# Seven block products in place of eight in both feed-forwards of a one-core transformer kernel

## The chip, the core and the metric

One core of a Trainium2 chip runs the whole program. The metric is the device time of one execution in microseconds; lower is better.

## The reference, cut to what matters

Two stages work on x of 512 tokens by 1024 columns in float32: two layers with three kinds of attention, a short convolution and gates, then a block with a feed-forward, a mixer with dilated and block-selected attention, cross attention over 256 memory rows, and a second feed-forward. The change touches the two feed-forwards alone (D_FF is 2816):

```python
def swiglu(x, w_gu, w_down):
    gu = x @ w_gu
    g, u = jnp.split(gu, 2, axis=-1)
    return (jax.nn.silu(g) * u) @ w_down

x = x + 0.5 * swiglu(rms_norm(x, g_ffn1[layer]), w_ffn1_gu[layer], w_ffn1_down[layer])
```

## The kernel before

Activations lie transposed: 128 partitions hold 128 columns of the model, and the free axis the 512 tokens. A matrix of weights is a stream of slots of 128 x 1024 words (eight blocks of 128 x 128), loaded by SyncE into a ring of four slots. Each float32 value is held as a rounded high part and a low part (the rest), and each product of two matrices is three matmuls: high by high, high weights by low values, low weights by high values (products, L1006; the matmul is L1013). ScalarE rounds a slot into whi (make_high, L1736), VectorE or GpSimd subtracts to get wlo in place in the ring (make_low, L2201 on VectorE, L759 on GpSimd).

A feed-forward (ffn, L1398 on TensorE, L1998 on ScalarE, L2601 on VectorE) has 44 up jobs, g and u in turn for each of 22 chunks of D_FF: eight chunks of 128 model columns, three matmuls of 512 tokens each, summed in one of two PSUM banks (proj). VectorE scales g by the norm's factor R (L2285), ScalarE takes the tanh (L2007), VectorE makes the gate (L2624), multiplies by u out of the bank (L2628) and by R (L2631); ScalarE rounds the result (inner_hi, L2010), VectorE makes inner_lo (L2642). Then 8 down jobs sum 22 chunks of inner each and are added to xT with a factor of 0.25 (residual, L2279). Squares of xT for the next norm go to ScalarE (L1732) and their sum to GpSimd (L771). GpSimd has no weights to split in the feed-forwards: on_pool names only slots of the layers and of the mixer.

Each engine runs its own list of instructions in order and waits on counters (semaphores) that others raise: job_done when a job's last matmul ends, job_free when its bank has been read, lo_ready when the low part of the weights is there. Jobs alternate between the two banks, so the reading of one bank lies beside the next job, which takes 5.4 us. SyncE reloads a ring slot when the job that used it is done (slot_used, L622).

## Time and profile before

| | before |
|---|---|
| time, median of 3 runs | 1786.37 us (1785.3 to 1786.94) |
| profiled execution, span | 1785.4 us |
| TensorE busy | 1776.4 us (99%) |
| VectorE busy | 1062.3 us (59%) |
| ScalarE busy | 750.5 us (42%) |
| GpSimd busy | 407.3 us (23%) |
| DMA | 165.53 MB, mean 93 GB/s |

The profile is of one execution. Busy time of an engine is the time in which it had an instruction under way; a matmul's recorded duration is longer than the distance from one start to the next, since they are pipelined. PE is TensorE, DVE is VectorE, ACT is ScalarE, POOL is GpSimd, SP is SyncE.

### The profile page before, as it was taken

What the parts mean: (1) busy time and instruction counts of PE and PEld (TensorE: products, weight loads), DVE (VectorE), ACT (ScalarE), POOL (GpSimd) and SP (SyncE); (2) the same over time, 40 slices, a digit from 0 to 9 for tenths busy, and PEclk for the clock granted to TensorE, in tenths of its full rate; (3) what the DMA queues carried; (4) which work ended last, traced back from release to release, by engine and by line L of the source; (5) the groups of instructions that cost most, each with busy time, mean ns of one, the idle gap of its engine ahead of it and who ended that gap; (6) DMA issues with size and microseconds to landing.
All of it is one profiled execution on the core that took longest, in us unless ns stands there. A gap on an engine that the chain in (4) does not pass through costs nothing.

```text
span 1785.4 us, 25187 instructions
## 1 busy us (share of the span) xinstructions
PE 1776.4 (99%) x9274; PEld 1437.2 (80%) x9274; DVE 1062.3 (59%) x2106; ACT 750.5 (42%) x1386; POOL 407.3 (23%) x248
## 2 busy tenths in 40 slices
PE   9999999999999999999999999999999999999998
PEld 7767778776777888888888878879888888888887
DVE  5888777588877665445433445555756654555333
ACT  6464654446454533223222455545444322232222
POOL 4544553455354310000000232220200200000000
PEclk9999999999999999999999999999999999999999
DMA  5422222322212343333333422323321333333332
GB/s 188 125 81 70 60 59 85 97 81 83 67 53 60 96 138 102 95 94 94 106 106 104 150 60 83 95 72 107 95 73 55 92 101 94 94 94 101 99 106 94
DMA packets 49765, 165.53 MB, mean 93 GB/s; under 512 B 5640, under 2 KB 6152, under 8 KB 49672
## 3 DMA queue, kind: packets, MB, share of 16 engines
q1 hardware_dynamic: 48376, 161.47, 30.2%
q10 hardware_dynamic: 1296, 2.84, 0.4%
q8 instruction: 56, 0.92, 0.2%
q14 instruction: 37, 0.30, 0.1%
HBM read 162.12 MB, written 2.17 MB: 92 GB/s over the span
## 4 chain that ended last, share of the span: by engine, by line
PE 97%; DVE 1%; ACT 1%; issue 0%; POOL 0%; DVEq 0%; POOLq 0%
PE proj L1013 78%; PE turned L1302 2%; PE o L1326 2%; PE score L1276 2%; PE turned L1530 1%; PE proj L1460 1%; PE o L1556 1%; PE score L1521 1%; PE proj L1453 1%; PE score L1285 1%; PE o L1652 1%; PE turned L979 1%; PE score L1641 1%; PE score L1163 0%; PE proj L991 0%; PE turned L998 0%
## 5 line engine op out<-in xcount | busy, mean ns | idle before, releaser
L1013 PE MATMUL proj<-hhi,whi 128*128 128x512 f32 x1456 | 580.2, 399 | 0.6 <-DVE tanh L2285 0.3
L1013 PE MATMUL proj<-hhi,wlo 128*128 128x512 f32 x1456 | 568.1, 390 | 0.0
L1013 PE MATMUL proj<-hlo,whi 128*128 128x512 f32 x1456 | 567.3, 390 | 0.0
L1736 ACT ACTIVATE whi<-ring 128x1024 fp32r<-128x1024 f32 x279 | 295.2, 1058 | 622.7 <-PE proj L1013 614.4
L2201 DVE TENSOR_TENSOR wlo<-ring,whi 128x1024 fp32r<-128x1024 f32 x199 | 243.1, 1222 | 164.8 <-ACT whi L1736 164.5
L1013 PEld LDWEIGHTS proj<-hhi,whi 128*128 128x128 f32 x1456 | 274.3, 188 | 59.4 <-issue 6.6
L1013 PEld LDWEIGHTS proj<-hhi,wlo 128*128 128x128 f32 x1456 | 273.4, 188 | 58.8
L1013 PEld LDWEIGHTS proj<-hlo,whi 128*128 128x128 f32 x1456 | 274.0, 188 | 52.8
L759 POOL TENSOR_TENSOR wlo<-ring,whi 128x1024 fp32r<-128x1024 f32 x80 | 194.7, 2435 | 372.6 <-ACT whi L1736 372.0
L771 POOL TENSOR_TENSOR prob<-prob 128x512 f32<-128x512 f32 x36 | 56.6, 1574 | 873.9 <-ACT prob L1732 873.9
L1762 ACT ACTIVATE prob<-prob,negmax 128x256 f32<-128x256 f32 (+3 forms) x208 | 114.4, 552 | 65.5 <-DVE negmax L2274 64.1
L1013 PE MATMUL proj<-inner_hi,whi 128*128 128x512 f32 x352 | 136.9, 389 | 0.0
L1013 PE MATMUL proj<-inner_lo,whi 128*128 128x512 f32 x352 | 136.9, 389 | 0.0
L1013 PE MATMUL proj<-inner_hi,wlo 128*128 128x512 f32 x352 | 136.9, 389 | 0.0
L2274 DVE CUSTOM_DVE_ANT_0 prob<-score,arena 128x256 f32<-128x256 f32 (+3 forms) x208 | 92.7, 482 | 62.1 <-PE turned L1530 55.3
L2285 DVE TENSOR_TENSOR tmp<-proj,R 128x512 f32<-128x512 f32 x48 | 33.2, 691 | 121.1 <-PE proj L1013 118.8
L1013 PE MATMUL proj<-yhi,whi 128*128 128x512 f32 x245 | 96.7, 395 | 0.1
L1013 PE MATMUL proj<-yhi,wlo 128*128 128x512 f32 x245 | 95.6, 390 | 0.0
L1013 PE MATMUL proj<-ylo,whi 128*128 128x512 f32 x245 | 95.3, 389 | 0.0
L2628 DVE TENSOR_TENSOR tmp<-tmp,proj 128x512 f32<-128x512 f32 x44 | 30.3, 689 | 103.7 <-PE proj L1013 103.5
L1943 ACT ACTIVATE pT<-turned 128x128 f32<-128x128 f32 (+3 forms) x96 | 38.5, 434 | 102.8 <-PE turned L1302 102.1
L1013 PEld LDWEIGHTS proj<-inner_lo,whi 128*128 128x128 f32 x352 | 66.1, 188 | 13.8
(334 smaller groups left out, 2426.1 us busy)
## 6 DMA issues: line engine op xcount, KB each, us to landing
ring<-wstream SPq DMA_DIRECT2D x287, 512.0 KB, 3.6
arena<-lines SPq DMA_DIRECT2D x28, 256.0 KB, 5.5
arena<-x ACTq DMA_DIRECT2D x4, 512.0 KB, 5.9
out<-arena SPq DMA_DIRECT2D x8, 256.0 KB, 2.9
arena<-mem SPq DMA_DIRECT2D x1, 1024.0 KB, 9.4
ring<-wstream ACTq DMA_DIRECT2D x2, 256.0 KB, 7.3
arena<-hot SPq DMA_DIRECT2D x2, 80.0 KB
par<-params ACTq DMA_DIRECT2D x2, 74.0 KB, 1.9
```

What stands on the lines that cost most here:

```text
L759: return pool.tensor_tensor(rounded(wlo[:, s, :]), ring[:, s, :], whi[:, h, :], ALU.subtract)
L771: pool.tensor_tensor(sq[:, 3, :], sq[:, 0, :] if c == 1 else sq[:, 3, :], sq_last if c == KC - 1 else sq[:, c % 3, :], ALU.add).then_inc(s ...
L1013: mm = pe.matmul(b, rounded(w), rounded(rhs(v, k)), start=(first and n == 0 and p == 0), stop=(last and n == len(blocks) - 1 and p == 2))
L1276: mm = pe.matmul(score[b][:, 0:W], rounded(q_part[rows, pair, q]), rounded(k_part[rows, pair, 0:W]), start=first, stop=last)
L1302: mm = pe.transpose(turned[g % 2][:, kb * P:(kb + 1) * P], prob[:, (2 * s + n) % 4, kb * P:(kb + 1) * P], ident[:, :])
L1326: mm = pe.matmul(opsum[o % 2][h * HD:(h + 1) * HD, qb * P:(qb + 1) * P], v, pT[:, (g - 1 + h) % 4, kb * P:(kb + 1) * P], start=(kb == 0), ...
L1736: act.activation(rounded(dst), src, ACT.Copy, scale=scale).then_inc(ready, 1)
L1762: act.activation(prob[:, i, 0:W], prob[:, i, 0:W], ACT.Exp, bias=negmax[:, i:i + 1], scale=-1.0, accum_out=rowsum[:, i:i + 1] if total is ...
L1943: act.activation(pT[:, g % 4, 0:W], turned[g % 2][:, 0:W], ACT.Copy).then_inc(turn_out, 1)
L2201: dve.tensor_tensor(rounded(wlo[:, s, :]), ring[:, s, :], whi[:, h, :], ALU.subtract).then_inc(lo_ready, 1)
L2274: dve.tensor_tensor_reduce(prob[:, i, 0:W], src[:, 0:W], bias, 1.0, 3e38, ALU.add, ALU.min, negmax[:, i:i + 1]).then_inc(min_ready, 1)
L2285: return dve.tensor_tensor(dst, src, factors, ALU.mult)
```

## The change

Each feed-forward keeps its first four weight pairs (g and u of chunks 0, 4, 1, 5) as eight jobs of the old kind. The other 18 pairs and all of the down matrix go through 30 blocks, each a product of a 2 x 2 block matrix of weights (two slots) by a 2 x 2 block matrix of values: the tokens are cut into two halves of 256 (TS), the chunks of the summed axis into two halves. An up block has g and u of one chunk as its two rows and four chunks in each half; a down block has two output chunks as its rows, and 8, 8 or 6 of the 22 inner chunks as its summed axis (three parts, each four blocks). Such a product needs seven block products on sums of blocks where the plain form needs eight; each is 12 matmuls of 256 tokens (9 in the last part). In order they are the 1st, 7th, 6th, 4th, 5th, 2nd, 3rd:

- into bank R0 go the 1st, then on top the 6th, the 5th and the 3rd; into R2 the 7th and on top the 4th; into R1 the 2nd. Each bank has two copies, used by blocks in turn. Between two products of one bank its partial sum is read: r0_out counts these readings (after the 1st, after the 6th, after the 5th, after the 3rd), r2_p7_out and r2_out those of R2, r1_out that of R1.
- in an up block ScalarE copies the sums out after the 1st, 7th and 6th product (c1, c7, c2) and VectorE adds: gsum = c1 + R1, tmp = c7 + R0 and tmp = c2 + R2. In a down block VectorE adds each partial sum into xT (x_add, seven times 256 columns).
- for each block GpSimd makes four sums of weights of 512 columns and the low part of the slot of u (1024); ScalarE rounds g (1024), u (1024), two sums together (1024) and one more (512); VectorE makes the low parts of g in two halves (a_low), of the two sums (s12_low) and of the last one (s4_low).
- the values need sums of blocks too: for the normalised input once per feed-forward, on VectorE, GpSimd and ScalarE beside the first four pairs; for inner, when both chunks of a pair are there (pair_of), three sums on VectorE (512, 256, 256 columns), one rounding on ScalarE and one low part on VectorE of 7 x 256 columns each. This comes in 9 of the 18 up blocks and in the first down block of the third part, which comes after all up blocks.
- the normalised input is computed with R and the gain ahead of the blocks, so their results need no factor R.
- the loops in the engines' programs become written out blocks; some semaphores are merged; the second feed-forward's last steps, the order of the last chunks of xT (H_ORDER) and the loads of eight of the mixer's bias tiles move to fit.

The core of the diff; TensorE first waits and runs, then ScalarE's, then VectorE's turn of the loop for block J (q is J mod 2; before is block J - 1):

```diff
-B2_EARLY = 9
+B2_EARLY = 8
...
+FFN_STD = 4
+FFN_JOBS = 2 * FFN_STD
+FFN_UP = (0, 4, 1, 5, 2, 6, 3, 7, 8, 12, 9, 13, 10, 14, 11, 15, 16, 19, 17, 20, 18, 21)
+FFN_FAST = [("up", c) for c in FFN_UP[FFN_STD:9]] + [("down", 0, m) for m in range(KC // 2)] \
+    + [("up", c) for c in FFN_UP[9:17]] + [("down", 1, m) for m in range(KC // 2)] \
+    + [("up", c) for c in FFN_UP[17:]] + [("down", 2, m) for m in range(KC // 2)]
...
+                def weight_sums(J):
+                    G, q, n, half = g0 + J, J % 2, n0 + FFN_JOBS + 2 * J, fast_half(FFN_FAST[J])
+                    a11, a12, a21, a22 = (ring_part(n + i, part, half) for i in range(2) for part in range(2))
+                    pool.wait_ge(wload[(n + 1) % RING], 16 * ((n + 1) // RING + 1))
+                    if J >= 2:
+                        product_done(pool, 5, f, J - 2)
+                    pool.tensor_tensor(s_part(SX, q, 0, half), a21, a22, ALU.add).then_inc(sums_ready, 1)
+                    pool.wait_ge(wload[n % RING], 16 * (n // RING + 1))
+                    pool.wait_ge(sums_ready, 4 * G + 1)
+                    pool.tensor_tensor(a21, a11, a21, ALU.subtract).then_inc(sums_ready, 1)
+                    pool.tensor_tensor(s_part(SX, q, 1, half), s_part(SX, q, 0, half), a11, ALU.subtract).then_inc(sums_ready, 1)
+                    pool.wait_ge(w_hi, 4 * G + U_HI)
+                    both = slice(0, 2 * half * P)
+                    pool.tensor_tensor(rounded(wlo[:, (n + 1) % RING, both]), ring[:, (n + 1) % RING, both], hi_u[q][:, both],
+                                       ALU.subtract).then_inc(u_lo, 1)
+                    if J >= 2:
+                        product_done(pool, 3, f, J - 2)
+                    pool.wait_ge(sums_ready, 4 * G + 3)
+                    pool.tensor_tensor(s_part(SX, q, 2, half), a12, s_part(SX, q, 1, half), ALU.subtract).then_inc(sums_ready, 1)
...
+            for p in (1, 7, 6, 4, 5, 2, 3):
...
+                def fast(J, to, o, w_hi, w_lo, start, ks):
+                    for n, k in enumerate(ks):
+                        cols = slice(k * P, (k + 1) * P)
+                        hi, lo = operand(J, o, k)
+                        for p, (w, v) in enumerate(((w_hi, hi), (w_hi, lo), (w_lo, hi))):
+                            mm = pe.matmul(to, rounded(w[:, cols]), rounded(v), start=(start and n == 0 and p == 0), stop=False,
+                                           skip_group_check=True)
+                    return mm
...
+                def p3(J):
+                    G = g0 + J
+                    pe.wait_ge(w_lo, 4 * G + S4_LO)
+                    r0_read(pe, R0_U4, f, J)
+                    fast(J, R0[J % 2], B22, *s_parts(J, 2), False, blocks(J)).then_inc(fast_done, 1)
...
+                for J in range(FASTS):
+                    p1(J)
+                    p7(J)
+                    p6(J)
+                    p4(J)
+                    p5(J)
+                    p2(J)
+                    p3(J)
...
+                    if before[0] == "up":
+                        act.wait_ge(r1_out, G)
+                        act.activation(tanh[:, 1 - q, 0:TS], gsum[:, 1 - q, :], ACT.Tanh, scale=0.5).then_inc(tanh_ready, 1)
+                    if job[0] == "up":
+                        product_done(act, 1, f, J)
+                        if G >= 2:
+                            act.wait_ge(r1_out, G - 1)
+                        act.activation(c1[:, q, :], R0[q], ACT.Copy).then_inc(r0_out[q], 1)
+                    if J < FASTS:
+                        weights_high(J, "s4")
+                    if before[0] == "down" and before[1] == 2 and J < FASTS:
+                        finish_high(before, 0)
+                    if job[0] == "up":
+                        product_done(act, 7, f, J)
+                        if J >= 2:
+                            r0_read(act, R0_U4, f, J - 2)
+                        act.activation(c7[:, q, :], R2[q], ACT.Copy).then_inc(r2_p7_out, 1)
+                    if J + 1 < FASTS:
+                        weights_high(J + 1, "g")
+                    if before[0] == "up":
+                        product_done(act, 3, f, J - 1)
+                        act.activation(tanh[:, 1 - q, TS:S], R0[1 - q], ACT.Tanh, scale=0.5).then_inc(tanh_ready, 1)
+                    if job[0] == "up":
+                        product_done(act, 6, f, J)
+                        if G >= 2:
+                            act.wait_ge(r2_out, G - 1)
+                        act.activation(c2[:, q, :], R0[q], ACT.Copy).then_inc(r0_out[q], 1)
+                    if J + 1 < FASTS:
+                        weights_high(J + 1, "u")
+                        weights_high(J + 1, "s12")
+                    if before[0] == "down" and before[1] == 2 and J < FASTS:
...
+                        pair = pair_of(before)
+                        last_down = max((n for n, b in enumerate(FFN_FAST) if b[0] == "down" and b[1] < before[1] // 8), default=None)
+                        inner_high(pair, d_place(before[1])[0], last_down)
...
+                def inner_sums(pair):
+                    done = 3 * (d0 + pair)
+                    dve.wait_ge(inner_done, f * FC + 2 * pair + 2)
+                    dve.tensor_tensor(raw[:, T1:T3 + 1:2, :], raw[:, B12::-(B12 - B22), :][:, 0:2, :], raw[:, B11:B12 + 1, :], ALU.subtract)\
+                        .then_inc(d_sum, 1)
+                    dve.wait_ge(d_sum, done + 1)
+                    dve.tensor_tensor(raw[:, T2, :], raw[:, T3, :], raw[:, B11, :], ALU.add).then_inc(d_sum, 1)
+                    dve.wait_ge(d_sum, done + 2)
+                    dve.tensor_tensor(raw[:, T4, :], raw[:, B21, :], raw[:, T2, :], ALU.subtract).then_inc(d_sum, 1)
...
+                def inner_low(pair, kk):
+                    dve.wait_ge(d_hi, d0 + pair + 1)
+                    dve.tensor_tensor(rounded(DL[:, kk, :]), raw[:, 0:7, :].rearrange("p a n -> p (a n)"), DH[:, kk, :], ALU.subtract)\
+                        .then_inc(d_lo, 1)
...
+                def x_add(c, t, src, ready):
+                    dve.scalar_tensor_tensor(x_block(c, t), src, 0.25, x_block(c, t), ALU.mult, ALU.add).then_inc(ready, 1)
...
+                def inner(J, before, tanhs, gates):
+                    G, q = g0 + J, J % 2
+                    dve.wait_ge(tanh_ready, tanhs)
+                    dve.scalar_tensor_tensor(tanh[:, 1 - q, TS:S], tanh[:, 1 - q, TS:S], 1.0, R0[1 - q], ALU.add, ALU.mult)\
+                        .then_inc(r0_out[1 - q], 1)
+                    r0_read(dve, R0_LAST, f, J - 1)
+                    dve.wait_ge(ffn_step, gates)
+                    dve.wait_ge(r2_out, G)
+                    dve.tensor_tensor(inner_at(before[1]), tanh[:, 1 - q, :], tmp[:, 1 - q, :], ALU.mult).then_inc(inner_done, 1)
+                    if pair_of(before) is not None:
+                        inner_sums(pair_of(before))
...
+                    if before[0] == "up":
+                        product_done(dve, 5, f, J - 1)
+                        dve.wait_ge(r2_p7_out, G)
+                        dve.tensor_tensor(tmp[:, 1 - q, TS:S], c7[:, 1 - q, :], R0[1 - q], ALU.add).then_inc(r0_out[1 - q], 1)
+                        product_done(dve, 4, f, J - 1)
+                        r0_read(dve, R0_U2, f, J - 1)
+                        dve.tensor_tensor(tmp[:, 1 - q, 0:TS], c2[:, 1 - q, :], R2[1 - q], ALU.add).then_inc(r2_out, 1)
+                        dve.wait_ge(tanh_ready, tanhs - 1)
+                        dve.scalar_tensor_tensor(tanh[:, 1 - q, 0:TS], tanh[:, 1 - q, 0:TS], 1.0, gsum[:, 1 - q, :], ALU.add, ALU.mult)\
                             .then_inc(ffn_step, 1)
...
+                    if before[0] == "down":
+                        product_done(dve, 5, f, J - 1)
+                        dve.wait_ge(r2_p7_out, G)
+                        x_add(2 * before[2] + 1, 1, R0[1 - q], r0_out[1 - q])
...
+                    if J == LAST_UP + 1:
+                        inner(J, before, tanhs, gates)
+                        a_low(J, 1)
+                        s4_low(J)
+                        inner_low(pair_of(before), d_place(before[1])[0])
...
+                    if job[0] == "down":
+                        product_done(dve, 1, f, J)
+                        x_add(2 * job[2], 0, R0[q], r0_out[q])
...
+                    if J < FASTS and J != LAST_UP + 1:
+                        a_low(J, 1)
+                        s4_low(J)
+                    if job[0] == "down":
+                        product_done(dve, 7, f, J)
+                        x_add(2 * job[2] + 1, 1, R2[q], r2_p7_out)
+                    if before[0] == "up" and J != LAST_UP + 1:
+                        inner(J, before, tanhs, gates)
+                    if before[0] == "down":
...
+                        a_low(J + 1, 0)
...
+                        s12_low(J + 1)
...
+                    if pair_of(before) is not None and J != LAST_UP + 1:
+                        inner_low(pair_of(before), d_place(before[1])[0])
+                    if f == 0 and J < 4:
+                        norm_first(2 * J)
+                        norm_first(2 * J + 1)
+                    if job[0] == "up":
+                        product_done(dve, 2, f, J)
+                        r0_read(dve, R0_P1, f, J)
+                        dve.tensor_tensor(gsum[:, q, :], c1[:, q, :], R1[q], ALU.add).then_inc(r1_out, 1)
```

## Rows read from the trace of the kernel before

**Rows 1.** The page of the kernel before: span, engines, TensorE's clock in forty slices
```profile
span 1785.4 us, 25187 instructions
...
PE 1776.4 (99%) x9274; PEld 1437.2 (80%) x9274; DVE 1062.3 (59%) x2106; ACT 750.5 (42%) x1386; POOL 407.3 (23%) x248
...
PEclk9999999999999999999999999999999999999999
```

**Rows 2.** Chain that ended last, in order: start, us, engine, what, count
```profile
644.06 353.60 PE proj L1013 x1560
...
1226.75 5.38 PE proj L1460 x45
...
1340.47 1.43 PE score L1641 x12
```

**Rows 3.** Stretches: window, busy us of PE, PEld, DVE, ACT, POOL, granted clock, DMA share, GB/s
```profile
200.00:220.00 20.00, 20.00 (x127) 15.77 (x126) 13.53 (x35) 10.74 (x31) 9.14 (x5) 0.91 0.10 28
640.00:1000.00 360.00, 360.00 (x1593) 298.20 (x1593) 173.72 (x209) 107.91 (x129) 10.19 (x9) 1.00 0.35 103
```

**Rows 4.** VectorE groups by form: tiles, shape, count, busy us, mean ns, idle before
```profile
L2201 DVE TENSOR_TENSOR wlo<-ring,whi 128x1024 fp32r<-128x1024 f32 x199 | 243.1, 1222 | 164.8 <-ACT whi L1736 164.5
...
L2285 DVE TENSOR_TENSOR tmp<-proj,R 128x512 f32<-128x512 f32 x48 | 33.2, 691 | 121.1 <-PE proj L1013 118.8 <-ACT R L1758 2.3
...
L2624 DVE SCALAR_TENSOR_TENSOR tmp<-tanh,tmp 128x512 f32<-128x512 f32 x44 | 30.1, 685 | 0.0
...
L2279 DVE SCALAR_TENSOR_TENSOR xT<-proj,xT 128x512 f32<-128x512 f32 x39 | 26.8, 688 | 29.8 <-PE proj L1013 28.8 <-PE proj L1612 1.0
...
L2274 DVE CUSTOM_DVE_ANT_0 prob<-score,arena 128x256 f32<-128x256 f32 x64 | 24.6, 421 | 19.1 <-PE turned L1530 17.7 <-PE score L1641 1.3
```

**Rows 5.** ScalarE groups by form
```profile
L1736 ACT ACTIVATE whi<-ring 128x1024 fp32r<-128x1024 f32 x279 | 295.2, 1058 | 622.7 <-PE proj L1013 614.4 <-PE proj L1460 5.2 <-PE proj L1612 2.6
...
L2010 ACT ACTIVATE inner_hi<-tmp 128x512 f32 x40 | 25.3, 632 | 23.0 <-DVE tmp L2631 23.0
...
L1769 ACT ACTIVATE pT<-turned 128x256 f32<-128x256 f32 x32 | 10.5, 381 | 25.5 <-PE turned L1530 25.5
```

**Rows 6.** GpSimd groups by form
```profile
L759 POOL TENSOR_TENSOR wlo<-ring,whi 128x1024 fp32r<-128x1024 f32 x80 | 194.7, 2435 | 372.6 <-ACT whi L1736 372.0
...
L791 POOL TENSOR_TENSOR wlo<-ring,whi 128x512 fp32r<-128x512 f32 x2 | 2.6, 1288 | 0.2
```

**Rows 7.** In order of time around 700.5: a job's last matmul and its two readers
```profile
700.11 0.39 PE L1013 MATMUL proj<-hhi,wlo 128*128 128x512 f32 x1
...
700.54 1.06 ACT L1736 ACTIVATE whi<-ring 128x1024 fp32r<-128x1024 f32 x1 [3.86 <-PE proj L1013]
...
700.62 0.69 DVE L2628 TENSOR_TENSOR tmp<-tmp,proj 128x512 f32<-128x512 f32 x1 [2.50 <-PE proj L1013]
```

**Rows 8.** In order of time, VectorE and GpSimd from 1007
```profile
1007.78 2.40 POOL L759 TENSOR_TENSOR wlo<-ring,whi 128x1024 fp32r<-128x1024 f32 x1 [7.42 <-ACT whi L1736]
...
1008.25 2.48 DVE L2719 TENSOR_TENSOR klo<-arena,khi 128x512 fp32r<-128x512 f32 x1 [0.38 <-ACT khi L1736]
```

**Rows 9.** In order of time, VectorE and GpSimd from 292: who gets the next turn
```profile
292.97 1.45 DVE L2209 SCALAR_TENSOR_TENSOR hlo<-xT,gnext,hhi 128x512 fp32r<-128x512 f32 x1 [0.25 <-ACT hhi L1736]
...
292.33 1.54 POOL L771 TENSOR_TENSOR prob<-prob 128x512 f32<-128x512 f32 x1 [24.20 <-ACT prob L1732]
293.83 1.73 POOL L903 TENSOR_TENSOR tanh<-tanh 128x512 f32<-128x512 f32 x1
```

**Rows 10.** TensorE in order of time around 208: thin work, then a 512-column matmul
```profile
205.38 1.84 PE L979 MATMUL proj<-halves,arena 128*128 128x2 f32 x16
...
211.22 0.63 PE L1013 MATMUL proj<-hlo,whi 128*128 128x512 f32 x1
```

**Rows 11.** The longest wait of TensorE
```profile
PE turned L963 <- POOL mhalf L745: 1.4, 1, 1.4
```

**Rows 12.** Transfers by form: KB each, median us to landing
```profile
ring<-wstream SPq DMA_DIRECT2D x287, 512.0 KB, 3.6
```

More of the change, by code:

```diff
@@ L135, in stream_of @@
 def stream_of(n):
-    if not PAIR_AT <= n < FFN2_AT:
+    for at in (FFN1_AT, FFN2_AT):
+        if at <= n < at + FFN_SLOTS:
+            return at + FFN_TAKE[n - at]
+    if n < FFN1_AT:
         return n
@@ L159, in is_split @@
         return n % LAYER_SLOTS not in RAW
-    return True
+    return not any(at + FFN_JOBS <= n < at + FFN_SLOTS for at in (FFN1_AT, FFN2_AT))
 def on_pool(n):
@@ L1559, in pv2 @@
                 mm.then_inc(pv_done, 2)
[L1561 to L1562 removed]
+            for k in H_ORDER:
+                pair_chunk("Q0", k, h_there(N_MIX), H_ORDER)
             for k in range(KC):
```

674 lines of the change are left out of this document (467 added, 207 removed).

## Prediction

> **What bounds the kernel now.** I read the page first: one core, a span of 1785.4 us, TensorE busy for 1776.4 of it at a granted clock of nine tenths or more in every slice [rows 1]. TensorE's longest wait is 1.4 us [rows 11]. So TensorE is the bound, without a gap to close, and only fewer or shorter matmuls can help. Next the chain of waits: 1560 matmuls of a feed-forward follow one another in 353.60 us, 0.2267 us each at 512 columns [rows 2]. Per feed-forward there are 44 up jobs of 8 chunks and 8 down jobs of 22 chunks, three matmuls each: 1584, or 359.1 us. Over the first of them VectorE is busy for 173.7 of 360 us, ScalarE for 107.9, GpSimd for 10.2 [rows 3]; there is idle time to spend.
>
> **TensorE's own work.** After the change 8 up jobs keep 24 matmuls at 512 columns: 192. The other 18 weight pairs and 8 of 12 down blocks take 7 products of 4 chunks and 3 matmuls, 84 at 256 columns; the last 4 down blocks have 3 chunks, 63. That is 26 x 84 + 4 x 63 = 2436. A 256-column matmul with its own weights takes 1.43 / 12 = 0.1192 us, or 5.38 / 45 = 0.1196 [rows 2]; I take 0.1193, not half of 0.2267. So 192 x 0.2267 + 2436 x 0.1193 = 334.1 us: 25.0 us less, 50.1 in both feed-forwards. An eighth of the changed part (359.1 - 43.5) would be 39 us; the half-width matmuls give 14 of it back.
>
> The Trainium skill, page "TensorE: Matmul & The Clock Gate", section "Wait — 56ns, not 53.3ns?", puts a warm matmul at its columns over 2.4 GHz and about 2.5 ns. By it 256 columns would take 109 ns, and TensorE's work would fall by some 49 us more than by my rows; the rows show 119 ns, so I keep those.
>
> **The new queues.** The products of a block run one after the other, each 12 x 0.1193 = 1.43 us, from 0: 1st to 1.43, 7th to 2.86, 6th to 4.3, 4th to 5.7, 5th to 7.2, 2nd to 8.6, 3rd to 10.0. Three of them add up in one bank, and between them the partial sum is read out. The reader starts 0.04 to 0.12 us after a matmul's end, and that end is 0.28 us or so behind the last start, so 0.2 to 0.3 us behind the next product's first slot [rows 7]. ScalarE's copies (c1, c7, c2) take 0.38 us [rows 5] and come within the product in between. The reading before the 3rd product does not: VectorE does it (c7 + R0) at the top of its next turn of the loop, behind everything of this turn and behind gsum, which waits for the 2nd product. The 3rd product waits for that reading.
>
> Prices on VectorE: 0.42 us at 256 columns, 0.69 at 512, 1.22 at 1024 [rows 4], so by the same slope 2.02 at 1792. ScalarE: 0.63 at 512, 1.06 at 1024 [rows 5], 1.70 at 1792. GpSimd: 1.29 at 512, 2.4 at 1024 [rows 6].
>
> *Without any contention.* An up block whose predecessor did not complete an inner pair: gsum starts at 8.6 + 0.28, ends 9.3, reading ends 9.7: TensorE waits 1.15 us. With a completed pair: ScalarE ends c7 at 3.45, the next weights' high part at 4.5, the second tanh at 4.9; then on VectorE gate 0.42, product 0.69, three sums 1.6, to 7.7; ScalarE rounds 1792 columns to 9.5 while VectorE makes two low parts (0.69 and 1.22) to 9.6; its 1792-column low part ends at 11.7, gsum 12.1, reading 12.55. TensorE waits 4.0 us. A down block waits 1.1 us in the same way (two additions behind the 2nd product). This alone, 9 x 4.0 + 9 x 1.15 + 8 x 1.1 for the blocks of four chunks and about 33 for the last four, is 88 us per feed-forward against 25 saved.
>
> *Contention.* Now VectorE and GpSimd. While GpSimd ran its 2.40 us subtraction from 1007.78, a VectorE subtraction of 512 columns begun at 1008.25 took 2.48 us in place of 0.69: it ended 0.55 us after GpSimd's end, as if it had not started before [rows 8]. From 292 the two take turns: GpSimd's add of 1.29 takes 1.54 and 1.73 behind VectorE's, VectorE's 1.45 in place of 0.75 [rows 9]. VectorE operations that read a bank keep their time (0.691 and 0.688 in the mean [rows 4]), so it is those with two SBUF operands that give way. Before, GpSimd had 10 us of work in a feed-forward. After, each block has 4 x 1.29 + 2.4 = 7.6 us on it, all on SBUF operands. VectorE's two-operand work in a pair-completing block is a low half 0.69 three times (two of the g weights, one of the 4th sum), the pair of sums 1.22, product 0.69, three inner sums 1.6, inner low 2.02 and a gate 0.42: 8.0 us. The two don't overlap.
>
> Worked through for such a block: the sums on VectorE begin at 6.0, and the low part of u, 2.35 on GpSimd, is ready at 6.1. In turns: sum to 6.7, u low to 9.05, sum 9.35, 4th weight sum 10.6, sum 10.9, first sum of the next weights 12.15, g low 12.7, GpSimd 13.95, pair low 15.0, GpSimd 16.25, inner low 18.15, gsum 18.5, reading 18.9. The 3rd product starts near 18.95 in place of 8.6: 10.35 us of waiting, 9 times, 93 us. In the other up blocks the same turns (u low to 8.9, pair low to 10.0, gsum and reading to 10.75) make it 2.2 us, 9 times, 20 us. Down blocks: the addition of the 7th product stands behind two low parts that each wait for GpSimd, which makes the 4th product 1.2 to 2.7 us late, and 1.1 at the end: 3.2 us, 8 times, 26 us. The first down block of the third part needs all inner pairs, and VectorE's and ScalarE's chain for the last pair stands ahead of its 1st product: 12 us. The last four, with 7.5 us of products but about 12 us of work under turns (squares on GpSimd among it), wait 4.5 us each: 18 us. The entry (operand sums, 2048-column parts) I put at 5 us, from below nothing to 10. Sum 174 us; the first feed-forward has 8 more normalisations before gsum, 5 us. Both: 354 us.
>
> *The clock.* After 1.84 us of near-empty matmuls at 205.38 a 512-column matmul took 0.63 us in place of 0.39 [rows 10], at the 1.2 GHz level, and the stretch from 200 to 220 has 0.91 of the clock in the mean: 0.09 x 20 = 1.8 us lost [rows 3]. Ten waits of over 8 us per feed-forward, each 1.7 us: 34 us in all, 0 to 100 as bounds, since every shorter wait might do it too, and a slower TensorE start is partly hidden behind ScalarE.
>
> **Costed at nothing:** loads (two slots of 3.6 us [rows 12] per 10 us or more; a slot of g is there some 4 us after the 2nd product, 12.6 us into a block, before its sum comes up in turn; if it is late, the turns shift by at most 1.3 us); the later bias loads (the mixer first needs eight, issued during the last down blocks); ScalarE's 6.6 us per block. In the final norm nothing moves by over 1 us.
>
> **Sum.** 1785.4 - 50 + 354 + 34 = 2123, and the median of the runs shown lies 1 us above the profiled span: 2124 us, 18.9% slower. The time outside the feed-forwards (about 1067 us) stays.
>
> The Trainium skill, page "SBUF — State Buffer", section "SBUF: two separate sides", speaks against the change: the port pair that VectorE and GpSimd share is locked for a whole instruction, and the other blocks fully. If the two merely shared bandwidth the price would lie between the two sums above; the rows of 1007 and 292 show blocking.
>
> **Rivals.** (1) Queue order alone: the turns cost little, since VectorE's and GpSimd's work falls into different stretches. For it: GpSimd's parts are only 7.6 of 11 to 14 us. Against it: the u low part and the inner sums become ready within 0.1 us of each other. It gives 1785 - 50 + 2 x 88 + 5 and up to 20 of clock: 1915 to 1940 us. (2) Faster: VectorE finishes a turn of its loop within the block, so the 3rd product waits for nothing; then 1786 - 50 = 1736 us, to 1780 with small gaps. It decides at 10.0 us from one reading to the next; VectorE's own work in a pair-completing block is 9.7 us before any wait, which speaks against it. (3) The clock stays at the lower level for much of both feed-forwards, as products come in bursts: a quarter of the 668 us of products at half speed is 167 us, of which 34 are counted above: some 2250 us, 2220 and over. (4) The change doesn't do what it says (as many matmuls as before): the counts in the diff exclude it.
>
> **Chances.** Forecast, 2000 to 2220: 0.70. Rival 1: 0.16. Rival 2: 0.06. Rival 3: 0.07. Rest 0.01. The range 1920 to 2220 leaves out rivals 2 and 3 and a part of rival 1. A measurement of this kernel tells 0.2% from no change: faster 0.06, same 0.01, slower 0.93.
>
> **What would show it.** After, in the chain of waits, products in stretches of 12 at 1.43 us; TensorE's waits led by VectorE's addition into tmp and by x adds; VectorE's two-operand groups with means well above 0.69 and 1.22, bank readers at 0.42; GpSimd busy some 450 us more; granted clock below 1 in the feed-forwards. Wrong if VectorE's groups keep their means (rival 1), or if TensorE stays at 99% (rival 2).

## The result, and the profile after

| | before | after |
|---|---|---|
| time, median | 1785.84 us (1785.09 to 1786.94) | 2172.44 us (2170.83 to 2174.93) |
| profiled execution, span | 1785.4 us | 2172.9 us |

The kernel became slower: 1.216 times the time of before (95% interval 1.2145 to 1.218), 386.6 us more. The forecast was 2124, with a range from 1920 to 2220.

The page of after, its head and the lines of TensorE, VectorE, GpSimd and the clock over 40 slices (the answer to [rows 1]):

```profile
span 2172.9 us, 30356 instructions
PE 1844.8 (85%) x11362; PEld 1594.0 (73%) x11362; DVE 1433.0 (66%) x2517; ACT 893.9 (41%) x1640; POOL 969.2 (45%) x560
PE   9999999999997668667758999999996667667757
PEclk9999999999998889779878999999998789879868
```

TensorE fell from 99% to 85% busy, and its slices below 9 are the two feed-forwards. GpSimd has 562 us more, where the prediction had said some 450. The waits of TensorE in the whole of after: what it waited for, us in all, times, longest:

```profile
PE score L1577 <- DVE tmp L3093: 217.3, 36, 9.7
PE score L1577 <- DVE xT L3059: 31.5, 24, 5.3
PE score L1577 <- issue: 19.9, 2, 10.2
PE proj L1577 <- DVE xT L3059: 19.3, 19, 2.4
PE proj L1158 <- DVE wlo L2552: 13.9, 8, 2.9
PE score L1577 <- ACT c L2344: 10.9, 2, 5.7
PE score L1577 <- DVE hlo L3037: 7.2, 2, 3.6
```

Before, the longest was 1.4 us [rows 11]. The first line is the reading ahead of the 3rd product (tmp = c7 + R0), once in each of the 36 up blocks, and it is more than half of all waiting. VectorE's groups by form (busy us, mean ns of one, idle before), first two with both operands in SBUF, then two that read a bank:

```profile
L2974 DVE TENSOR_TENSOR wlo<-ring,whi 128x512 fp32r<-128x512 f32 x52 | 70.7, 1360 | 1.0 <-ACT whi L1991 1.0
L3004 DVE TENSOR_TENSOR raw<-raw 128x256 f32<-128x256 f32 x22 | 44.0, 1999 | 0.8
L3093 DVE TENSOR_TENSOR tmp<-c,score 128x256 f32<-128x256 f32 x36 | 14.7, 408 | 0.0
L3065 DVE SCALAR_TENSOR_TENSOR tanh<-tanh,score 128x256 f32<-128x256 f32 x36 | 15.1, 419 | 48.1 <-ACT tanh L2358 48.1
```

The first took 1360 ns, where operations of 512 columns took about 690 before; the second took 1999, where 256 columns took about 420 [rows 4]. The bank readers kept their time. GpSimd's own groups grew as well (1288 at 512 columns before [rows 6]):

```profile
L1033 POOL TENSOR_TENSOR SX<-SX,ring 128x512 f32<-128x512 f32 x52 | 105.5, 2029 | 0.0
L1041 POOL TENSOR_TENSOR SX<-ring,SX 128x512 f32<-128x512 f32 x52 | 76.2, 1465 | 0.0
```

Now one up block of the second feed-forward whose predecessor completed no pair, VectorE and GpSimd in order of time (start, length, and in brackets the idle time before and what ended it):

```profile
1862.53 2.75 POOL L1036 TENSOR_TENSOR wlo<-ring,hi_extra 128x1024 fp32r<-128x1024 f32 x1 [8.67 <-ACT hi_extra L1991]
1865.24 1.26 POOL L1041 TENSOR_TENSOR SX<-ring,SX 128x512 f32<-128x512 f32 x1
...
1862.33 0.68 DVE L2974 TENSOR_TENSOR wlo<-ring,hi_extra 128x512 fp32r<-128x512 f32 x1
1866.60 2.20 DVE L2982 TENSOR_TENSOR SX_lo<-SX,HS 128x1024 fp32r<-128x1024 f32 x1 [3.59 <-POOL SX L1041]
1868.72 0.41 DVE L3158 TENSOR_TENSOR gsum<-c,o 128x256 f32<-128x256 f32 x1
1869.05 0.41 DVE L3093 TENSOR_TENSOR tmp<-c,score 128x256 f32<-128x256 f32 x1
```

VectorE stands idle for 3.59 us ahead of the low part of the two sums (s12_low, L2982), though these sums have long been there: s12_low also waits for GpSimd's 4th sum (L1041), which stands behind the low part of u. gsum, the reading and the 3rd product (1869.61) come behind that. The wait on the 4th sum was in the source and was not in my working. GpSimd itself stood idle for 8.67 us first, for the high part of u, which ScalarE makes behind its copy after the 6th product.

TensorE's side of the wait before it: the 3rd product's first matmuls (start, recorded length).

```profile
1853.54 0.56 PE L1577 MATMUL score<-hhi,HS 128*128 128x256 f32 x1 [8.36 <-DVE tmp L3093]
1853.89 0.42 PE L1577 MATMUL score<-hlo,HS 128*128 128x256 f32 x1
1854.11 0.41 PE L1577 MATMUL score<-hhi,SX_lo 128*128 128x256 f32 x1
...
1856.88 0.32 PE L1577 MATMUL score<-hhi,whi 128*128 128x256 f32 x1
1857.04 0.28 PE L1577 MATMUL score<-hlo,whi 128*128 128x256 f32 x1
1857.16 0.28 PE L1577 MATMUL score<-hhi,wlo 128*128 128x256 f32 x1
```

After the wait of 8.36 us the matmuls start 0.21 us apart (1854.11 to 1856.88 is 13 of them), and then 0.12 us apart. The first spacing is that of 256 columns at 1.2 GHz (256 / 1.2 = 213 ns).

### Where the 386.6 us are

From the starts of all 4872 matmuls of the blocks in order of time I took three sums: 0.12 us for each; where the next start is 0.135 to 0.3 us later, the excess is time at the lower clock; above 0.3 us it is waiting. The entry is how much later the first matmul of the blocks starts than the matmul in the same place did before: 692.64 against 678.58, and TensorE had been 0.43 us ahead when the feed-forward began, so 14.5 us; in the second feed-forward it is 14.7.

| both feed-forwards | predicted | after |
|---|---|---|
| TensorE's own work | -50 | -47 |
| entry, beyond its matmuls | +10 | +29 |
| waits in the blocks | +344 | +321 |
| lower clock in the blocks | +34 | +84 |
| sum | +338 | +387 |

The steady lengths from block to block (from one reading of the 2nd product's bank to the next) were 20.2 to 20.9 us where an inner pair is completed, 16.1 to 16.7 in the other up blocks and 12.1 to 12.4 in down blocks; the first blocks behind a change between up and down differ (14.2 for an up block, 14.9 to 16.4 for a down block). TensorE's own work in each is 10.08 us.

### The profile page after: what moved, and what is told of

It reads as the page before. It is cut to its first block, busy times and chain, and to the rows that moved or that the text cites. A ratio compares the mean times of both kernels' runs of the same rounds, so it can differ in the third digit from the quotient of the medians.

```text
span 2172.9 us, 30356 instructions
## 1 busy us (share of the span) xinstructions
PE 1844.8 (85%) x11362; PEld 1594.0 (73%) x11362; DVE 1433.0 (66%) x2517; ACT 893.9 (41%) x1640; POOL 969.2 (45%) x560
## 4 chain that ended last, share of the span: by engine, by line
PE 66%; DVE 11%; issue 11%; POOL 7%; DMA 4%; ACT 1%; DVEq 0%; POOLq 0%; ACTq 0%
PE proj L1158 32%; PE score L1577 12%; PE proj L1577 4%; DMA ring<-wstream 4%; PE o L1577 2%; POOL SX L1041 2%; POOL SX L1033 2%; PE turned L1447 2%; POOL ring L1032 2%; PE o L1471 2%; DVE wlo L2974 1%; PE score L1421 1%; POOL wlo L1036 1%; DVE SX_lo L2989 1%; PE turned L1780 1%
## 5 line engine op out<-in xcount | busy, mean ns | idle before, releaser
L1158 PE MATMUL proj<-hhi,whi 128*128 128x512 f32 x880 | 359.4, 408 | 14.5 <-DVE wlo L2552 13.9
L1158 PE MATMUL proj<-hhi,wlo 128*128 128x512 f32 x880 | 346.2, 393 | 0.0
L1158 PE MATMUL proj<-hlo,whi 128*128 128x512 f32 x880 | 345.5, 393 | 0.0
L1991 ACT ACTIVATE whi<-ring 128x1024 fp32r<-128x1024 f32 (+1 forms) x219 | 229.5, 1048 | 259.7 <-PE proj L1158 191.6
L1577 PE MATMUL score<-hhi,HS 128*128 128x256 f32 x144 | 62.6, 434 | 217.3 <-DVE tmp L3093 217.3
L1158 PEld LDWEIGHTS proj<-hhi,whi 128*128 128x128 f32 x880 | 167.6, 190 | 54.2 <-issue 23.6
L1158 PEld LDWEIGHTS proj<-hhi,wlo 128*128 128x128 f32 x880 | 166.7, 189 | 36.8
L1158 PEld LDWEIGHTS proj<-hlo,whi 128*128 128x128 f32 x880 | 167.4, 190 | 30.5
L2982 DVE TENSOR_TENSOR SX_lo<-SX,HS 128x1024 fp32r<-128x1024 f32 (+1 forms) x60 | 87.5, 1458 | 97.0 <-POOL SX L1041 97.0
L2552 DVE TENSOR_TENSOR wlo<-ring,whi 128x1024 fp32r<-128x1024 f32 x79 | 106.6, 1350 | 25.6 <-ACT whi L1991 25.1
L1991 ACT ACTIVATE HS<-SX 128x1024 fp32r<-128x1024 f32 (+1 forms) x120 | 98.4, 820 | 51.6 <-POOL SX L1041 43.0
L1033 POOL TENSOR_TENSOR SX<-SX,ring 128x512 f32<-128x512 f32 (+1 forms) x60 | 117.9, 1964 | 0.0
```

The lines of the kernel that those rows point to most:

```text
L1033: pool.tensor_tensor(s_part(SX, q, 1, half), s_part(SX, q, 0, half), a11, ALU.subtract).then_inc(sums_ready, 1)
L1158: mm = pe.matmul(b, rounded(w), rounded(rhs(v, k)), start=(first and n == 0 and p == 0), stop=(last and n == len(blocks) - 1 and p == 2))
L1577: mm = pe.matmul(to, rounded(w[:, cols]), rounded(v), start=(start and n == 0 and p == 0), stop=False, skip_group_check=True)
L1991: act.activation(rounded(dst), src, ACT.Copy, scale=scale).then_inc(ready, 1)
L2552: dve.tensor_tensor(rounded(wlo[:, s, :]), ring[:, s, :], whi[:, h, :], ALU.subtract).then_inc(lo_ready, 1)
L2982: dve.tensor_tensor(rounded(s_pair(SX_lo, q, half)), s_pair(SX, q, half), s_pair(HS, q, half), ALU.subtract)\
```

## Experiments

The table lists for each kernel the time, its ratio to the kernel before on the same chip, and the two sums as above (waits in the blocks, time lost at the lower clock). In e3 and e12 the dummy matmuls are counted as waiting. e1, e10 and e13 leave out the weight sums or part of them, so they compute other results and only their times are of use.

| kernel | time | ratio (95%) | waits | clock |
|---|---|---|---|---|
| after | 2172.4 | 1.216 (1.2145 to 1.218) | 321 | 84 |
| e1 GpSimd writes only | 2090.7 | 1.171 (1.1675 to 1.1743) | 233 | 86 |
| e2 early reading | 2017.6 | 1.130 (1.1241 to 1.1358) | 184 | 61 |
| e3 filled gaps | 2114.6 | 1.184 (1.1809 to 1.1877) | 319 | 27 |
| e4 2nd ahead of 5th | 2183.9 | 1.223 (1.2195 to 1.2266) | 331 | 84 |
| e5 4th sum ahead of u's low part | 2071.7 | 1.160 (1.1548 to 1.1645) | 241 | 61 |
| e7 no GpSimd | 2007.3 | 1.124 (1.1203 to 1.1268) | 189 | 50 |
| e8 no GpSimd, early reading | 1940.4 | 1.086 (1.083 to 1.0893) | 128 | 44 |
| e9 early reading, 4th sum first | 1993.3 | 1.116 (1.1115 to 1.12) | 177 | 52 |
| e10 narrow sums, early reading | 1881.7 | 1.053 (1.0502 to 1.0563) | 86 | 27 |
| e12 e8 with filled gaps | 2046.2 | 1.145 (1.1419 to 1.1486) | 259 | 22 |
| e13 e10, inner low part late | 1862.0 | 1.042 (1.0394 to 1.0455) | 68 | 24 |
| e14 e8, inner low part late | 1918.2 | 1.074 (1.0708 to 1.077) | 121 | 29 |

### Is it the turns with GpSimd? (e1)

The turns are VectorE and GpSimd holding each other up: one runs while the other stands. Here each of GpSimd's five operations becomes a fill, two memsets of its columns and then one or two of 256:

```diff
-                    pool.tensor_tensor(s_part(SX, q, 0, half), a21, a22, ALU.add).then_inc(sums_ready, 1)
+                    fill(s_part(SX, q, 0, half), half * P, sums_ready)
...
```

> GpSimd's five operations on the weights of each block are replaced by memsets of about the same length (two of the whole width and one or two of 256 columns, each waiting for the one before), so the weights' sums and the low part of u are not computed; every wait stays. GpSimd is as busy as before, but reads nothing. Theory A (VectorE and GpSimd take turns on operations with two SBUF operands): VectorE's low parts return to 0.69 us at 512 columns and 1.22 at 1024, the chain in a pair-completing block loses three to five turns of 1.3 us, and the time falls by 100 to 160 us, to 2010 to 2070. Theory B (order and length of the queues alone, turns matter little): VectorE's means stay above 1.0 at 512 columns or the time stays above 2120 us.

```profile
L2986 DVE TENSOR_TENSOR wlo<-ring,whi 128x512 fp32r<-128x512 f32 x52 | 35.5, 684 | 1.1 <-ACT whi L2003 1.1
L2994 DVE TENSOR_TENSOR SX_lo<-SX,HS 128x1024 fp32r<-128x1024 f32 x52 | 63.6, 1224 | 138.7 <-POOL SX L1029 138.7
```

By form again, as above. VectorE's groups are back at 684 and 1224 ns while GpSimd is nearly as busy as in after (900.7 us, 969.2 there; a fill in place of a sum takes 2 x 0.525 + 0.312 = 1.36 us, the one of u's low part 2.53), and the time falls by 82 us. So the turns are real, and it is GpSimd's reading that takes them. But they are worth 82 us, less than the 100 to 160 expected here, and not the 178 us by which the prediction's two sums differed (2 x 88 without, 354 with). And without them the kernel still takes 305 us more than before, where the sum without contention had 129 to 154. The second line shows a part of what stays: 138.7 us of idle time of VectorE ahead of s12_low, ended by GpSimd's fill in place of the 4th sum.

### The wait on the 4th sum (e5)

```diff
+                    if J >= 2:
+                        product_done(pool, 3, f, J - 2)
+                    pool.wait_ge(sums_ready, 4 * G + 3)
+                    pool.tensor_tensor(s_part(SX, q, 2, half), a12, s_part(SX, q, 1, half), ALU.subtract).then_inc(sums_ready, 1)
                     pool.wait_ge(w_hi, 4 * G + U_HI)
...
-                    pool.tensor_tensor(s_part(SX, q, 2, half), a12, s_part(SX, q, 1, half), ALU.subtract).then_inc(sums_ready, 1)
```

> GpSimd makes the 4th sum of weights before the low part of u (before, it came after it, and VectorE's low part of the two sums also waits for it). The trace of the changed kernel shows VectorE idle for 90.8 us in all before that low part, released by GpSimd's 4th sum; my working had left this wait out. If that edge is a cause of its own, up blocks that complete no pair lose most of their 4.3 us of waiting, and the time falls by 60 to 110 us, to 2060 to 2110. If it only hides behind other things (turns, ScalarE), the time stays above 2140.

Measured: 101 us less; the first line of the waits fell from 217.3 to 144.0. Exchanging two instructions on GpSimd brought more than taking the turns away. VectorE's s12_low by form, in after and in e5:

```profile
L2982 DVE TENSOR_TENSOR SX_lo<-SX,HS 128x1024 fp32r<-128x1024 f32 x52 | 78.1, 1503 | 90.8 <-POOL SX L1041 90.8
...
L2982 DVE TENSOR_TENSOR SX_lo<-SX,HS 128x1024 fp32r<-128x1024 f32 x52 | 121.4, 2335 | 18.0 <-ACT HS L1991 17.4 <-POOL SX L1037 0.6
```

Its idle time for GpSimd's sum is gone (90.8 to 0.6 us), and a part of it comes back as a turn with the low part of u (1503 to 2335 ns). The missed wait is shown. Not all of the 101 us need be VectorE's: ScalarE's rounding of the same 4th sum also waited for it, 40.1 us in after and 5.3 in e5, and no run separates the two.

### The late reading (e2, e9)

In `inner`, ahead of the inner sums, in place of the top of the next turn of the loop:

```diff
+                    if read:
+                        third_read(J)
                     if pair_of(before) is not None:
                         inner_sums(pair_of(before))
+
+                def third_read(J):
...
+                    product_done(dve, 5, f, J)
+                    dve.wait_ge(r2_p7_out, G + 1)
+                    if job[0] == "up":
+                        dve.tensor_tensor(tmp[:, q, TS:S], c7[:, q, :], R0[q], ALU.add).then_inc(r0_out[q], 1)
+                    else:
+                        x_add(2 * job[2] + 1, 1, R0[q], r0_out[q])
...
```

> VectorE's reading of the bank after the 5th product (c7 + R0, or the addition to xT) is moved from the top of the next turn of its loop into this block's turn: behind the product of gate and u in an up block, behind the low part of the two sums in a down block. So the 3rd product no longer waits for gsum nor for the inner low part. Theory B (the queue order is what costs): the waits before the 3rd product nearly vanish and nothing takes their place, time under 1960 us. Theory A (VectorE and GpSimd have more locked work than the block lasts): the wait moves to the 1st or 6th product, which wait for low parts, and about half of the gain is left: 2020 to 2100 us.

> Early reading and the 4th sum first, GpSimd kept at its work. Two-operand work of VectorE and GpSimd together is 15.6 and 12.0 us per up block, 13.8 in the mean, and 10.9 in a down block. If that is now the bound: up blocks of 14 us, 1950 to 1990 us. If it comes out under 1900, turns matter less than I think; above 2010, the two edges overlap and the second gives nothing.

e2 is 155 us faster than after, just beyond the lower end of theory A's 2020 to 2100. TensorE's waits are no longer led by the reading:

```profile
PE score L1577 <- issue: 51.9, 6, 12.8
PE score L1577 <- ACT c L2344: 41.6, 22, 5.4
PE score L1577 <- DVE wlo L2974: 28.5, 12, 3.1
```

Yet 184 us of waiting remain, now for low parts and for ScalarE's first copy; the first line is six waits at the first down block of each part, up to 12.8 us. With e5's exchange on top (e9) only 24 us more go, less than expected: 1993 against 1950 to 1990. The two steps (155 and 101 us alone) do not add up; that both shorten the same chain is my reading of it.

### How much is the clock? (e3)

Dummy matmuls into a bank that nothing reads:

```diff
                     p2(J)
+                    if FFN_FAST[J][0] == "up":
+                        closes = J > 0 and FFN_FAST[J - 1][0] == "up" and d_place(FFN_FAST[J - 1][1])[1]
+                        for n in range(60 if closes else 30):
+                            pe.matmul(turned[1][:, 0:TS], rounded(hhi[:, n % KC, 0:P]), rounded(hhi[:, n % KC, 0:TS]),
+                                      start=True, stop=True, skip_group_check=True)
                     p3(J)
```

> TensorE runs matmuls of 256 columns into an unused bank between the 2nd and the 3rd product of each up block, 60 (7.2 us at full clock) where the block before completed a pair and 30 (3.6 us) elsewhere; their results are not used. The waits measured there are 8.4 and 4.3 us. If the lower clock after each wait costs about 117 us (387 more in all, less 320 of waits, plus 50 of shorter products), the granted clock goes above 0.97 and the time falls by 60 to 110 us, to 2060 to 2110. If the slow matmuls are hidden behind VectorE's and ScalarE's chain, the clock rises too, but the time stays within 20 us of 2172.

The dummy matmuls (7.2 and 3.6 us) fit into the waits of 8.4 and 4.3 us: counted as waiting, they leave the waits at 319 us (321 in after). The kernel does more work and is 58 us faster, at 2114.6 just above the expected 2060 to 2110; the excess of slow matmuls falls from 84 to 27 us, by 57. So the lower clock after the waits is on the path, and of the rows of the table above it is the one furthest from its forecast. The chain of waits of this kernel, where TensorE resumes:

```profile
1861.64 3.10 PE score L1577 x24
1864.74 1.44 PE proj L1577 x12
```

And the same place in two blocks of after:

```profile
1869.61 4.60 PE score L1577 x24
...
1906.42 5.38 PE score L1577 x24
```

### The order of the 2nd and 5th product (e4)

The 2nd product ahead of the 5th, so that the sum for gsum is in its bank 1.4 us earlier.

> The 2nd product goes ahead of the 5th (order 1st, 7th, 6th, 4th, 2nd, 5th, 3rd), nothing else. The 3rd product waits for VectorE's reading after the 5th, which stands behind all of VectorE's turn and gsum in either order, and VectorE comes to gsum 3 to 8 us after the 2nd product. So up blocks should not change; in down blocks the wait before the 3rd product is 0.7 in place of 1.1 us. All theories of mine: 2150 to 2180 us. Above 2200 or under 2130 would say that the order of these two is a cause by itself.

Measured: 2183.9, 11.5 us slower than after and just above the expected 2150 to 2180. An earlier 2nd product brings nothing: gsum and the reading stand behind VectorE's and GpSimd's queues, not behind that product. Of the 11.5 us, 9.5 are in the waits for VectorE's reading (217.3 to 226.8); why they grew was not followed.

### Without GpSimd (e7, e8)

The five operations of each block go to VectorE, at 0.69 and 1.22 us; e8 adds the early reading.

> GpSimd's five operations per block all move to VectorE (the four sums of the next block ahead of the low part of g, in the wait for the 7th product; the low part of u before that of the two sums). VectorE gets 3.8 us more work per block, GpSimd none. The late reading before the 3rd product stays. If taking turns and GpSimd's slower operations are what costs, the time falls although VectorE has more to do: about 14.5 us for a pair-completing block (20.1 now) and 12.8 for the others (16.1 now), 1960 to 2010 us. If VectorE's own length is what costs, it rises by 3.8 x 60 = 228 us at most, to 2200 to 2400.

> As no_gpsimd, and with the early reading before the 3rd product. What is left is VectorE's own work: 13.5 us in a pair-completing block, 10 in other up blocks, 9.2 in down blocks, against 10.0 us of products. If nothing else stands in the way: 11.8 us per up block in the mean, 1860 to 1900 us. With waits that I don't foresee: up to 1960. Under 1786 would overturn the reading that VectorE's work is now the bound.

e7 takes 165 us off: an engine that does all the work alone, one operation after the other, is faster than two that take turns and wait for each other. It takes away three things at once, the turns, GpSimd's longer operations (1.29 and 2.4 us) and the wait on its 4th sum, and does not say which brought how much. e8 missed its range (1860 to 1900) by 40 us, within the 1960 allowed for waits not foreseen. Its up blocks did come near VectorE's own work, 9.5 and 13.3 us from 1691.56 on (11.4 in the mean), 10.6 and 13.5 elsewhere. What I had left out is the rest: down blocks of 12.2 us, the entry, and the changes between the parts.

### Fewer columns, same instructions (e10, e13)

From the third block on, GpSimd's four sums and ScalarE's high and VectorE's low parts of them are cut to 64 columns:

```diff
+                    if J >= 2:
+                        a11, a12, a21, a22, *s_all = (v[:, 0:64] for v in (a11, a12, a21, a22, *s_all))
...
-                    pool.tensor_tensor(s_part(SX, q, 0, half), a21, a22, ALU.add).then_inc(sums_ready, 1)
+                    pool.tensor_tensor(s_all[0], a21, a22, ALU.add).then_inc(sums_ready, 1)
...
```

> The early reading of the 3rd experiment's kind (the 5th product's bank read ahead of the inner sums), and from the third block of each feed-forward on, GpSimd's four weight sums, ScalarE's high parts and VectorE's low parts of these sums cover 64 columns of each 512 only; the rest of the sums and the result that hangs on it are left out. All matmuls, all waits and all other operations stay. VectorE then has some 9 us of work in a pair-completing block and 5 in another, GpSimd 3.6. Theory A (TensorE's own work is 50 us less, as the sum of my prediction has it, and what took its place is the amount of element work behind the readings): 1786 - 50 + 32 of waits at the entry + 2 x 10 to 20 at the first down block of the third part + 10 to 40 of clock, so 1790 to 1860, TensorE busy about 1750 at the full clock. Theory B (the order of readings holds TensorE up whatever the amount of work): 1900 or more, with up blocks still 11 us or longer.

1881.7 lies between the two theories. Against e2, which has the same early reading, fewer columns bring 136 us, and 95 us above before remain: down blocks ran at 10.1 us, TensorE's own pace, but two up blocks took 22.1 us. The chain of waits shows why, from VectorE's reading (start, us, what):

```profile
1645.18 0.42 DVE tmp L3091
1645.60 1.12 DVE raw L3010
1646.74 0.44 DVE raw L3013
1647.20 0.44 DVE raw L3015
1647.67 1.71 ACT DH L1994
...
1651.34 0.43 DVE gsum L3176
...
1652.11 0.38 ACT c L2347
1652.49 0.14 issue
1652.62 1.67 PE score L1580 x12
```

The inner sums, ScalarE's 1792-column high part and VectorE's low part of it stand ahead of gsum. The tanh of gsum stands ahead of ScalarE's first copy (c1), and the 6th product waits for the copy. The engines are idle for parts of it; it is the order that costs. e13 moves one instruction:

```diff
-                    if pair_of(before) is not None and J != LAST_UP + 1:
+                    if pair_of(before) is not None and J != LAST_UP + 1 and job[0] != "up":
                         inner_low(pair_of(before), d_place(before[1])[0])
...
                         dve.tensor_tensor(gsum[:, q, :], c1[:, q, :], R1[q], ALU.add).then_inc(r1_out, 1)
+                        if pair_of(before) is not None and J != LAST_UP + 1:
+                            inner_low(pair_of(before), d_place(before[1])[0])
```

> The kernel with narrow weight sums (1881.7, in which part of the sums is left out), and in up blocks VectorE's low part of the inner values (1792 columns, which waits for ScalarE's high part) stands behind gsum in place of ahead of it. In that kernel two up blocks take 22.1 us in place of 2 x 10.08, with 27.0 us of waits for ScalarE's copy c1: gsum came 3.3 us after the 2nd product's end, behind the low part, and c1 stands behind the tanh of gsum. Theory A (this place in the order is all that still holds TensorE up there): two up blocks take 20.2 us, the waits for c1 fall below 8 us, the time by 25 to 40 us to 1842 to 1857. Theory B (another chain of about the same length lies beside it): the two blocks keep over 21.5 us and the time stays over 1870.

> The kernel with all weight sums on VectorE and the early reading (1940.4), with the same move: the inner low part behind gsum in up blocks. Nothing is left out. Two up blocks take 23.4 us there, and VectorE's own work in them is 22.8 (9.5 and 13.3). Theory A (VectorE's amount of work bounds the up blocks): at best 0.6 us less for each of 18 such pairs of blocks, so 1925 to 1945. Theory B (the order, and not the amount, still costs several us): under 1915.

e13: 1862.0, 20 us less, with two up blocks in 20.8 us (11.4 and 9.4) and not the 20.2 expected; the range was missed by 5 us. The first copy still costs 13.6 us, in 4 waits, all in the first two blocks of the two feed-forwards. The largest waits left, 37.3 us in six, stand at the first down block of each part, the longest (11.7 us) at the third part, which needs all inner pairs. Its sum closes on before: -47 of work, +30 entry (taken as above), +68 of waits, +24 of clock is +75, and 1862.0 - 1785.7 is 76.3.

e14: 1918.2, 22 us less than e8, faster than theory A allowed and slower than B. Two up blocks took 22.2 us there, and VectorE had its next instruction under way within 0.15 us all through them: it was busy for 21.49 us of the 22.2 from 1700. Its lines, from one reading of the 2nd product's bank to the next (start, length):

```profile
1698.27 2.02 DVE L3012 TENSOR_TENSOR DL<-raw,DH 128x1792 fp32r<-128x1792 f32 x1
...
1709.13 0.42 DVE L3175 TENSOR_TENSOR gsum<-c,o 128x256 f32<-128x256 f32 x1
...
1720.16 0.41 DVE L3175 TENSOR_TENSOR gsum<-c,o 128x256 f32<-128x256 f32 x1
1720.49 2.02 DVE L3012 TENSOR_TENSOR DL<-raw,DH 128x1792 fp32r<-128x1792 f32 x1
```

So in e14, the fastest kernel here that computes everything, VectorE is the bound of the up blocks, with 11.1 us a block in the mean against 10.08 of TensorE. Before, these chunks cost TensorE 48 x 0.2267 = 10.88 us. A better order alone cannot make this form win: 11.1 is already more than 10.88, before the entry, the down blocks and the clock. A better split is not excluded: ScalarE was busy for only 11.66 of those 22.2 us and GpSimd for none, and no run gave a part of VectorE's work to ScalarE, or only a part of the sums to GpSimd.

### Filling again (e12)

> The kernel with all weight sums on VectorE and the early reading (1940.4), with 60 matmuls of 256 columns into a free bank between the 2nd and the 3rd product of pair-completing up blocks and 30 in the other up blocks. Theory A (there VectorE is the bound of the up blocks, 11.4 us of work in the mean, and the clock's loss lies inside TensorE's spare time): within 30 us of 1940, above or below, with a higher granted clock than 0.966. Theory B (what is left of the loss is TensorE at the lower clock level): at least 40 us faster, under 1900.

A miss for both theories: 106 us slower than e8. The blocks took 13.8 and 17.1 us, which is 10.08 and 30 or 60 times 0.12: the dummy matmuls were longer than the gaps and set the pace themselves. The loss at the lower clock did fall, from 44 to 22 us, but waits and dummies together rose from 128 to 259. So it does not decide between the theories; it shows that e8's other up blocks (9.5 to 10.6 us) had no gap to fill.

## Why the prediction was right, point by point

- **TensorE's work**: -50 predicted, -47 found. A product of 12 took 1.44 us where I had 1.43. By the Trainium skill's page "TensorE: Matmul & The Clock Gate", section "Wait — 56ns, not 53.3ns?", an estimate would be 12 x 109 ns, 1.31 us; the measurement decides, and it is that of [rows 2].
- **The reading ahead of the 3rd product**: right in place and in sum. I had 10.35 and 2.2 us for the two kinds of up blocks, 226 us in all. The trace has 8.36 and 4.26, and 217.3 us in all. The near agreement of the sum is luck: one kind was 2 us too long, the other 2 us too short. The turns were priced too high (e1 gives 82 us for all of them), and the wait of s12_low on the 4th sum was missed, which e5 prices at 101 us together with its share of the clock and ScalarE's wait for the same sum. (My two feed-forwards add up to 174 + 174 + 5 = 353, not 354.)
- **Contention**: the mechanism is shown (e1), but not its size. I had 176 us of waits without the turns and 178 more by them; e1 has 233 us of waits in the blocks without them, and they add 88 (82 in time). Adding whole turns one after another was too strict: VectorE was idle for long stretches (3.59 us in the block above), so fewer operations met than my list has; this explanation is read from that block and was not tested by itself.
- **Down blocks**: predicted 3.2 us of waiting on 10.0 of products, measured about 2.2 (12.1 to 12.4 in length). The first of the third part waited 10.2 us (12 predicted).
- **The entry**: 5 us per feed-forward predicted, with 10 as its upper bound, 14.5 and 14.7 found. In the first one TensorE waits 2.83, 1.84, 0.39 and 1.60 us for low parts of the wide jobs' weights, which took VectorE 3.00 and 3.40 us in place of 1.22 beside GpSimd's operand sums of 1024 columns, and 3.62 us ahead of the first block, where s12_low had waited 4.04 us for GpSimd's 4th sum. No run took these apart.
- **The clock**: 34 us predicted, 84 found, 58 of it confirmed by e3. I had counted ten waits of over 8 us at 1.7 each per feed-forward. Waits of 4.3 us cost as much: after that of 4.26 us the next 24 matmuls took 4.60 in place of 2.88 us, elsewhere 5.38. Of the 36 waits ahead of the 3rd product in up blocks 34 (of 3.4 us and more) were followed by 12 to 25 slow matmuls; two of 2.0 us by five. My upper bound of 100 held it.
- **Rivals**: order alone (1915 to 1940) fell by its own sign, VectorE's means above their alone times. But e1 shows that it named the larger part: with the turns gone the time is still 2090.7, so the order and the length of the queues, with what follows from them (entry and clock), cost more than the whole of my forecast without turns. The faster case fell with the 85%. The clock for much of the feed-forwards (2250) fell too: 84 us, not 167.
- **Loads costed at nothing**: the chain of waits of after passes through loads (3.45 us from 1881.44), but there it goes on with 9.24 us of "issue", in which GpSimd waits for ScalarE's high part of u; in these up blocks the load is early enough. In down blocks e5 took the low part of u (2.8 us) out of the way from a load to s12_low, and their length stayed at 12.1 to 12.4 us, so the loads cost nothing there that shows. GpSimd did wait for slots, 180.3 us in all ahead of its first two sums; what that costs at the changes between down and up blocks was not tried.

What was not tried: the seven products in the down blocks alone, with the old up jobs. Down blocks of four chunks a half took mostly 12.1 us and more wherever all sums were computed, against 10.88 for the same work before; only with part of the sums left out (e10, e13) did they reach 10.1.

## What to carry to other kernels

A product saved on the bound engine is paid for on the engines that make its sums: price the whole block on each of them first, and compare that with the old time of the bound engine, here 11.1 us of VectorE against 10.88 of TensorE. Then draw every wait of the source, not only those that the change speaks of: one sum made too late was worth 101 us, and one low part ahead of gsum 20. A reader that frees a bank for the bound engine belongs ahead of everything that can wait.

## What the runs showed of the hardware

- TensorE's matmuls of 256 columns start 0.12 us apart at the full clock and 0.213 at 1.2 GHz. The Trainium skill, page "TensorE: Matmul & The Clock Gate", section "Back-to-back issue gap", gives columns over 1.2 GHz for the lower level, and the trace agrees.
- In after, every wait of 3.4 us or more in the blocks was followed by 12 to 27 matmuls at the lower level, with 1.1 to 2.5 us lost. After waits of 0.5 to 1.6 us it was mostly one or two matmuls (in e10 12 of them took 1.67 in place of 1.44 us). In between it went both ways: in e8, after waits of 2.4 us, two slow matmuls from 838.42 on and 19 from 861.04 on.
- VectorE's operations with both operands in SBUF and GpSimd's that read SBUF hold each other up; they do not when GpSimd only writes. With GpSimd writing alone (e1), VectorE's two-operand subtraction of 512 columns took 684 ns; beside GpSimd's sums 1360, and a 256-column one 1999 in place of 420. Operations that read a bank kept 408 to 419 ns. The Trainium skill, page "SBUF — State Buffer", section "SBUF: two separate sides", says so, with the condition that GpSimd reads SBUF; e1 shows that condition at work. Both lose: one of GpSimd's 512-column sums took 2029 ns in the mean in place of 1288, behind VectorE's operations, more than the 1.54 and 1.73 us of [rows 9].
